# Projections of the next head placed inside a head's attention steps, in a one-core YOCO decoder step

## The reference

```python
k, v = split(rmsnorm(x, kv_norm) @ w_kv)            # 8 heads, keys of 2 x 64, values of 128
q = (rmsnorm(x, norm_mix[1]) @ w_q)                 # 8 heads, 2 maps of 64
for each head h, for both maps c:
    s = q[h, c] @ k[h, c].T * 64 ** -0.5 + bias[h]  # causal; sample rows see the cache and their new keys
    p[c] = softmax(s)
o = (p[0] - lam * p[1]) @ v[h]
o = rmsnorm(o, subln) * (1 - lam_init)
x = x + o @ w_o
x = x + conv_ffn(rmsnorm(x, norm_ffn[1]))
```

## Time and profile before

| | |
|---|---|
| median of 3 runs | 2920.72 us (2919.48 to 2922.08) |
| the profiled execution | 2921.39 us, of which its span is 2919.5 us |
| mean granted TensorE clock | 0.958 |
| PE busy | 2757.5 us (94%) |
| DVE, ACT, POOL busy | 1474.0, 651.8 and 801.0 us |
| keys, values and queries, after their norm | about 1239 to 1519 us of the span |
| attention | 1519 to 1941.3 us |

### The profile page before, as it was taken

One profiled execution on the slowest core, in us unless ns is written; L12 is line 12 of the kernel. 1 busy time (PEld: TensorE's weight loads), 2 busy tenths in 40 slices (PEclk: granted clock), 3 DMA queues, 4 the chain that ended last, 5 costly groups with the idle time before them and its releaser, 6 DMA issues.

```text
span 2919.5 us, 39213 instructions
## 1 busy us (share of the span) xinstructions
PE 2757.5 (94%) x16820; PEld 2678.5 (92%) x16820; DVE 1474.0 (50%) x2348; ACT 651.8 (22%) x946; POOL 801.0 (27%) x456
## 2 busy tenths in 40 slices
PE   5999999999999999899988989879999999999996
PEld 4998999999999999899987778779999999999995
DVE  6666454444445444711315666644544444444556
ACT  4444221111111111300103454432211111111111
POOL 2332333322233223222230011012222332233321
PEclk8999999999999999999997787889999999999998
DMA  3112211111111111123121212021111111111111
GB/s 125 39 42 64 84 44 44 44 51 44 44 44 46 49 44 44 62 84 140 66 83 56 97 56 102 30 101 48 45 45 44 44 45 51 44 44 44 47 48 66
DMA packets 44796, 171.06 MB, mean 59 GB/s; under 512 B 5221, under 2 KB 6821, under 8 KB 44238
## 3 DMA queue, kind: packets, MB, share of 16 engines
q1 hardware_dynamic: 39442, 139.93, 14.4%
q10 hardware_dynamic: 5180, 28.62, 2.6%
HBM read 141.77 MB, written 23.09 MB: 56 GB/s over the span
## 4 chain that ended last, share of the span: by engine, by line
PE 84%; DVE 8%; ACT 4%; issue 3%; POOL 1%; SPq 0%; ACTq 0%; DMA 0%; DVEq 0%; POOLq 0%
PE psum L629 74%; PE psum L865 2%; PE psum L844 2%; PE psum L888 2%; DVE line L1272 2%; DVE x L1338 1%; PE psum L817 1%; PE psum L877 1%; ACT line L1113 1%; ACT probs L1188 1%; DVE line L1313 1%; POOL w_lo L557 0%; DVE inverse_rms L1325 0%; DVE line L1293 0%; DVE xn_lo L1319 0%
## 5 line engine op out<-in xcount | busy, mean ns | idle before, releaser
L629 PE MATMUL psum<-xn_hi,w_hi 128*128 128x352 f32 x3648 | 795.8, 327 | 33.9 <-DVE xn_lo L1319 14.1
L629 PE MATMUL psum<-xn_lo,w_hi 128*128 128x352 f32 x3648 | 790.0, 324 | 0.0
L629 PE MATMUL psum<-xn_hi,w_lo 128*128 128x352 f32 x3648 | 789.6, 325 | 0.0
L553 POOL TENSOR_SCALAR w_hi<-w_raw 128x1024 fp32r<-128x1024 f32 x200 | 215.0, 1075 | 1770.2 <-PE psum L629 1684.4
L629 PEld LDWEIGHTS psum<-xn_hi,w_hi 128*128 128x128 f32 x3648 | 624.3, 190 | 37.6 <-issue 27.3
L629 PEld LDWEIGHTS psum<-xn_lo,w_hi 128*128 128x128 f32 x3648 | 629.2, 189 | 0.0
L629 PEld LDWEIGHTS psum<-xn_hi,w_lo 128*128 128x128 f32 x3648 | 623.0, 189 | 0.0
L557 POOL TENSOR_TENSOR w_lo<-w_raw,w_hi 128x1024 fp32r<-128x1024 f32 x200 | 512.6, 2563 | 16.7
L1338 DVE TENSOR_TENSOR x<-psum,x 128x1056 f32<-128x1056 f32 x208 | 261.3, 1256 | 240.6 <-PE psum L629 239.9
L1113 ACT ACTIVATE line<-line,columns 128x1072 f32<-128x1072 f32 x96 | 123.3, 1285 | 1062.0 <-DVE line L1295 1062.0
L1290 DVE TENSOR_TENSOR line<-psum,inverse_rms 128x704 f32<-128x704 f32 x104 | 92.7, 892 | 472.3 <-PE psum L629 472.2
(11 more groups left out here) (197 smaller groups left out, 2152.3 us busy)
## 6 DMA issues: line engine op xcount, KB each, us to landing
w_raw<-in_w SPq DMA_DIRECT2D x200, 512.0 KB, 3.5
k_pages<-in_cache_k SPq DMA_DIRECT2D x16, 512.0 KB, 4.6
v_pages<-in_cache_v SPq DMA_DIRECT2D x16, 512.0 KB, 5.4
scratch_line<-scratch_row ACTq DMA_DIRECT2D x1, 4608.0 KB, 19.8
x<-in_x ACTq DMA_DIRECT2D x8, 528.0 KB, 11.0
scratch_x<-x ACTq DMA_DIRECT2D x1, 4224.0 KB, 12.1
out_k<-k_t ACTq DMA_DIRECT2D x1, 4224.0 KB, 14.1
out_v<-line ACTq DMA_DIRECT2D x8, 528.0 KB, 2.6
```

The costliest lines, as they stand in the source:

```text
L553: pool.tensor_scalar(WHI[:, s], WRAW[:, s], 1.0, 0.0, ALU.mult, ALU.add).then_inc(w_hi, 1)
L629: last = pe.matmul(PS[:, 3 * (a % 2) + c, 0:CH], w[:, s, k, :], r[:, c * CH:(c + 1) * CH], start=start and first, stop=stop and final)
```

## The change

**The projections.** Units are reordered to query, key, value of one head after another. Only those of head 0's query and key run ahead of attention (`unit(U_A)`, `unit(U_A + 1)`). The other 22 are cut into single k tiles of one chunk: 528 *products* of three matmuls, all on one of the banks 0 and 1, which change after 8 products (`fill`). 16 products run first (`LEAD`), and then 9 in each step (`RATE`), in three groups of three between the step's other work. DVE reads a finished chunk out at two places of a step (`evac_chunks`) into `raw`, from which ACT makes the high parts and POOL the low ones. The second chunk after a finished one may not begin before that one is read (`raw_done`).

**The gains** of the norms are multiplied into the weights by POOL (`split_scaled`), one more two-input instruction of 128 x 1024 for each of the 24 units; `xn_hi` and `xn_lo` are x itself and are computed once. The round trip of queries and keys through `q_t` and `k_t` falls away.

**The steps** are 64, 8 for each head, with tiles in the order 0, 7, 1, 6, 2, 5, 3, 4. `scores` takes both maps by turns in each product. Scores have banks 2 to 5, and all else (transposes, values, sample work) takes banks 6 and 7 by turns in one fixed order (`ring_order`, `open_event`). The maximum and its negation become a minimum of negated scores, so L1727 falls away, and squares are summed by ACT tile by tile.

**Sample attention** treats all 8 sequences of one head at a time: 1 matmul with the new keys and 8 with the pages, three transposes, and 1 and 16 matmuls for the output. Its keys and values come in 32 DMAs of 64 KB for a head in place of 4 of 512 KB.

**The end.** Outputs of heads go to DRAM and come back into `xn_lo`, and the output projection of the first two units runs k tile by k tile (`project`) between the last steps' work.

```diff
-U_K = U_F0 + F_UNITS
-U_V = U_K + KT
-U_Q = U_V + KT
-U_O = U_Q + KT
+U_A = U_F0 + F_UNITS
+U_O = U_A + 3 * NH
...
+TILES = (0, 7, 1, 6, 2, 5, 3, 4)
+STEPS = NH * 8
+LEAD = 16
+RATE = 9
+PRODUCTS = (3 * NH - 2) * NCH * KT
...
+def ring_order():
+    order = []
+    for g in range(STEPS + 3):
+        h, t = divmod(g, 8)
+        if 2 <= g < STEPS + 2:
+            order += [("w", g - 2, b) for b in range(halves(g - 2))]
+        if g < STEPS and t == 2:
+            order += [("v", h, 0), ("v", h, 1), ("v", h, 2)]
+        if g < STEPS and t in (1, 3, 5):
+            order.append((("scores", "weights", "output")[t // 2], h))
+        if g >= 3:
+            order.append(("o", g - 3))
+        if g < STEPS and h and t >= 6:
+            order.append(("ot", h - 1, t - 6))
+        if g == STEPS:
+            order.append(("squares",))
+    return order + [("ot", NH - 1, 0), ("ot", NH - 1, 1)]
...
-        TILES = (0, 1, 2, 3, 4, 5, 6, 7)
-        SAMPLE_STEP = (1, 9)
...
+                pool.tensor_tensor(WRAW[:, s], WRAW[:, s],
+                                   COL[:, gain:gain + KT].unsqueeze(2).to_broadcast([P, KT, P]),
+                                   ALU.mult).then_inc(w_gain, 1)
+                pool.wait_ge(w_gain, n + 1)
+                pool.tensor_scalar(WHI[:, s], WRAW[:, s], 1.0, 0.0, ALU.mult, ALU.add
+                                   ).then_inc(w_hi, 1)
+                pool.wait_ge(w_hi, u + 1)
+                pool.tensor_tensor(WLO[:, s], WRAW[:, s], WHI[:, s].bitcast(F32), ALU.subtract
+                                   ).then_inc(w_lo, 1)
...
+            def low_qk(n):
+                h, k = divmod(n, 3)
+                hi, lo = ((QHI, QLO), (KHI, KLO))[k]
+                pool.wait_ge(qkh_done, 2 * h + k + 1)
+                pool.tensor_tensor(lo[h % 2][:, :], RAW[n % 2][:, 0:SEQ], hi[h % 2][:, :].bitcast(F32),
+                                   ALU.subtract).then_inc(qkl_done, 1)
...
+            def fill(n):
+                for j in range(pos[0], min(pos[0] + n, PRODUCTS)):
+                    q, k = divmod(j, KT)
+                    m, c = divmod(q, NCH)
+                    if j == 0:
+                        wait_read(pe, A_A)
+                    if q >= 2 and k == 0:
+                        pe.wait_ge(raw_done, q - 1)
+                    if c == 0 and k == 0:
+                        pe.wait_ge(w_lo, U_A + 2 + m + 1)
+                    s, cols = (U_A + m) % 2, slice(c * CH, (c + 1) * CH)
+                    pe.matmul(PS[:, q % 2, 0:CH], WHI[:, s, k, :], XNH[:, k, cols],
+                              start=(k == 0), stop=False)
+                    pe.matmul(PS[:, q % 2, 0:CH], WLO[:, s, k, :], XNH[:, k, cols],
+                              start=False, stop=False)
+                    last = pe.matmul(PS[:, q % 2, 0:CH], WHI[:, s, k, :], XNL[:, k, cols],
+                                     start=False, stop=(k == KT - 1))
+                    if k == KT - 1:
+                        last.then_inc(chunk_done, 1)
+                pos[0] = min(pos[0] + n, PRODUCTS)
...
+            def open_event(*e):
+                if EV[e] >= 2:
+                    pe.wait_ge(ev_free[EV[e] % 2], EV[e] // 2)
+                return bank(e)
...
+            def scores(g):
+                h, t = divmod(g, 8)
+                i, p = tile_of(g), h % 2
+                n = (i + 1) * P
+                if t == 0:
+                    pe.wait_ge(qkl_done, 2 * h + 2)
+                if g:
+                    pe.wait_ge(ttr_done, 2 * g)
+                for b in range(0, n, 512):
+                    w = min(512, n - b)
+                    for j, (q, k) in enumerate(((QHI, KHI), (QLO, KHI), (QHI, KLO))):
+                        for c in range(2):
+                            rows = slice(c * HD, (c + 1) * HD)
+                            last = pe.matmul(PS[:, 2 + 2 * c + b // 512, 0:w],
+                                             q[p][rows, i * P:(i + 1) * P], k[p][rows, b:b + w],
+                                             start=(j == 0), stop=(j == 2))
+                            if j == 2 and b + w == n:
+                                last.then_inc(s_done, 1)
...
+            def turn_weights(g):
+                pe.wait_ge(wc_done, g + 1)
+                for half in range(halves(g)):
+                    z = open_event("w", g, half)
+                    for b in range(4 * half, min(4 * half + 4, tile_of(g) + 1)):
+                        last = pe.transpose(PS[:, z, (b % 4) * P:(b % 4 + 1) * P],
+                                            PR0[g % 4][:, b * P:(b + 1) * P], IDENT[:, :])
+                    last.then_inc(ev_done, 1)
...
-                        for c in range(2):
-                            pe.wait_ge(ttr_done, hp * 32 + (2 * t + c + 1))
-                            rows = slice(c * HD, (c + 1) * HD)
-                            for b in range(0, n, 512):
-                                w = min(512, n - b)
-                                for p, (q, k) in enumerate(((QHI, KHI), (QLO, KHI), (QHI, KLO))):
-                                    last = pe.matmul(PS[:, 2 * c + b // 512, 0:w],
-                                                     q[s][rows, i * P:(i + 1) * P],
-                                                     k[s][rows, b:b + w],
-                                                     start=(p == 0), stop=(p == 2))
-                            last.then_inc(s_done, 1)
...
+            fill(LEAD)
+            for g in range(STEPS):
+                h, t = divmod(g, 8)
+                scores(g)
+                fill(RATE // 3)
+                if g >= 2:
+                    turn_weights(g - 2)
+                if t == 2:
+                    turn_values(h)
+                fill(RATE // 3)
+                if t == 1:
+                    sample_scores(h)
+                if t == 3:
+                    sample_weights(h)
+                if t == 5:
+                    sample_output(h)
+                if g >= 3:
+                    values(g - 3)
+                fill(RATE - 2 * (RATE // 3))
+                if h and t >= 6:
+                    turn_output(h - 1, t - 6)
+            turn_weights(STEPS - 2)
...
+            turn_weights(STEPS - 1)
+            pe.wait_ge(raw_done, PRODUCTS // KT)
+            pe.wait_ge(ttr_done, 2 * STEPS)
+            pe.wait_ge(osl_done, 1)
+            project(range(0, 2))
+            values(STEPS - 2)
+            project(range(2, 4))
+            values(STEPS - 1)
+            project(range(4, NH - 1))
+            turn_output(NH - 1, 0)
+            turn_output(NH - 1, 1)
+            project((NH - 1,))
+            for s in range(2, KT):
+                unit(U_O + s, A_O + s, release=(s == KT - 1))
...
+            def evac_chunks(upto):
+                for q in range(taken[0], upto):
+                    m, c = divmod(q, NCH)
+                    n = m + 2
+                    cols = slice(c * CH, (c + 1) * CH)
+                    if c == 0:
+                        line_free(n)
+                    dve.wait_ge(chunk_done, q + 1)
+                    if n % 3 == 0:
+                        dve.scalar_tensor_tensor(RAW[n % 2][:, cols], PS[:, q % 2, 0:CH], -HD ** -0.5,
+                                                 RINV[:, cols], MUL, MUL).then_inc(raw_done, 1)
+                    else:
+                        dve.tensor_tensor(RAW[n % 2][:, cols], PS[:, q % 2, 0:CH], RINV[:, cols], MUL
+                                          ).then_inc(raw_done, 1)
+                taken[0] = max(taken[0], upto)
...
+            for g in range(STEPS):
+                h, t = divmod(g, 8)
+                if g >= 4:
+                    output_rows(g - 4)
+                if t == 2:
+                    sample_biased(h)
+                if t == 4:
+                    sample_combined(h)
+                if t == 6:
+                    sample_rows(h)
+                biased(g)
+                evac_chunks(chunks_by(g, RATE // 3))
+                if g:
+                    combine(g - 1)
+                if t == 1:
+                    sample_biases(h)
+                if t == 3:
+                    sample_normalized(h)
+                if h and t == 4:
+                    variance(h - 1)
+                if h and t == 5:
+                    scaled(h - 1)
+                if g == STEPS - 2:
+                    wait_event_read(dve, "output", NH - 1)
+                    dve.memset(CARRY[:, 5:6], 0.0).then_inc(osm_done, 1)
```

1073 lines of the change are left out of this document (556 added, 517 removed).

## The result

The changed kernel takes 2786.72 us (median of 4 runs, 2785.28 to 2791.95) against 2921.14 us before (a fourth run is added to the three above): a ratio of 0.9545, 95% interval 0.953 to 0.9559. The prediction was 2798 us. On a second chip the same kernel took 2793.94 us (2790.20 to 2794.29), ratio 0.9567 (0.9554 to 0.958). The profiled execution took 2785.28 us with a span of 2783.5 us, 136.0 less than before.

The account below looks back on a forecast made before the run. PE, busy for 94% of the span, bounds the kernel; attention loses time to waits and a lowered clock. The changed stretch's terms sum to 629.0 us against 752.6; 123.6 saved from 2921.4 gives 2798 us, range 2760 to 2872.

Parts of the forecast that it names:

- leading products, first chunk's reading: Before attention's steps: 16 leading products take 7.8 us, and the first chunk's reading, which nothing covers, takes 2.
- seven heads: Attention heads with products: 70.7 us each (68.9 of PE work, 1.8 of waits and delays), 494.9 in all.
- step with the last 8 products: Attention's step holding the remaining 8 products, after the seven heads: 8.4 us.
- last seven steps: Attention steps with no products left run as before: 47.9 x 7/8 = 41.9, less 2 for maps' turns, 40 us.
- the end: After the last steps: 6 us wait, late passes 4.7, two output projection units 23.3, last turn 1, split 2.5: 37.5.
- the fourth step's 1 us for the sample's weights: In a head's fourth step PE wants the sample's weights before DVE has them ready; 1 us of wait shows.
- the copy's 0.3: In each head the third event of `v` makes PE wait 0.3 us for an ACT copy.
- the first rival: Heads with products: PE still waits for weights and rows; in full 84.0 us a head, 2891 us; chance 0.13.
- The second: Heads with products: the clock stays low, 2907 us at 0.82, 2847 halfway, taken as its time; chance 0.11.
- The third: Scores: taking maps by turns brings nothing, since they overlap already; 18 us back, 2816 us; chance 0.07.
- The fourth: Chunk readings on DVE come late behind POOL instructions; 66 chunks cost 169 us, 2967 us; chance 0.06.
- The fifth: Products: a chunk's matmuls on one bank each wait for the one before; 261 us more, 3059 us; chance 0.01.

Follow-up runs that it names:

- nine_at_once: The changed kernel with each step's nine products in one piece behind the scores and chunks read out at the step's end: 2830.16 us, ratio 0.9692.
- maps_in_order: The changed kernel with each step's scores taking all of the first map before the second, as the kernel before does: 2808.52 us, ratio 0.9624.

## Why the prediction was right, step by step

The mechanism was right: products between the pieces of a step cover the waits in the heads, and the clock stays up with them. The 2798 us were 11 too many, and that they are so near is in part luck: the heads came out 19 us below their term, and the last head and the end 11 above theirs.

| term | forecast us | measured us |
|---|---|---|
| first unit and norm gap | 25.1 | 25.0 |
| second unit | 13.3 | 13.4 |
| leading products, first chunk's reading | 9.8 | 7.7 |
| seven heads | 494.9 | 475.9 |
| step with the last 8 products | 8.4 | 6.3 |
| last seven steps | 40.0 | 44.9 |
| the end | 37.5 | 43.5 |
| sum | 629.0 | 616.7 |

**Heads, 19 us too high.** Head 0, which has no outputs of a head before it to turn, took 64.5, the others 68.5 to 68.7. The terms of head 2, each summed from the distances between starts: waits were put at 1.8 us and are 0; the fourth step's 1 us for the sample's weights and the copy's 0.3 did not show. Value passes were put at 0.12 each and cost 0.106 (7.66 for 72), and with the transposes and the sample's output it is 17.6 us for 19.3. Scores are 8.8, of which 0.7 is tile 3 at the low clock (1.58 us where four blocks took 0.91), so 8.1 for 9.2. The 216 matmuls of products take 38.4, of which 0.8 is the low clock (four starts 0.29 apart and not 0.16, and two entries that are longer by 0.1 and 0.2), so 37.6 for 36.7: a group's entry cost 0.11 us and not 0.07. The forecast had nothing for the clock, which cost 1.5. Together 70.7 - 1.8 - 1.7 - 1.1 + 0.9 + 1.5 = 68.5.

**The last head and the end, 11 us too low.** The last seven steps and the end, in the columns of the earlier trace rows:

```profile
1742.20:1787.10 44.90, 35.70 (x231) 27.84 (x230) 29.52 (x90) 29.27 (x71) 3.42 (x2) 0.87 0.46 180
1787.10:1830.60 43.50, 35.18 (x194) 33.76 (x194) 13.00 (x21) 9.88 (x21) 3.50 (x3) 0.83 0.17 58
```

The last seven steps were read off as seven eighths of an old head. That was right for PE's work (43.2 x 7/8 less 2 is 35.8, and it was busy for 35.7) and wrong for its waits: seven eighths of the old head's 4.7 idle us are 4.1, and here they are 9.2. 2.8 of them are for the sample's weights in the fourth step, 3.1 for rows. For the end it is the other way round. Its waits are 2.4, 3.0, 2.0 and 1.0, together 8.4, and the forecast gave 6 and 2.5 for the split. But its work took 35.1 us in place of 29.0: the clock is 0.83 there, and the forecast priced all of it at full clock.

**The rivals.** The chain stayed hidden; nine_at_once, where 18.9 us of waits come back, shows that it is hidden by the groups of three, which was the argument against the first rival. The second, a clock that stays low, is left as the 1.5 us a head at a clock of 0.98. The third is excluded by maps_in_order, where scores cost 2.3 us a head more. The fourth needed 1.87 us of stall a chunk and has one of 1.2 us in all; DVE is busy for 33 us of 68.5 in a head, as was worked out (ACT for 28.8, where about 35 were). The fifth: matmuls of a group start 0.16 us apart on one bank. The gain's multiplication on POOL, priced at 2.56 us, took 1.9.

**The rules.** That matmuls start in strict program order (the Trainium skill, TensorE: Matmul & The Clock Gate, The mechanism) would make the smaller tiles slower in maps_in_order; they were not. Its 2808.52 us lies nearer to the 2805 of four tiles than to the 2823 of eight; the total was taken on another chip and says little by itself, but the heads say it: 2.3 us each, all in the larger tiles.

## What to carry to other kernels

Work that depends on nothing around it is worth most when it is cut into pieces and put between two neighbours that hand a bank to each other: the same 72 products a head gave 475.9 us in 24 pieces, 511.0 in 8 and 534.0 in 3. A saving on the busiest engine counts in full only where nothing else is waited for, so cover the chain first and shorten the engine's work then (for the same edit, 2.3 us a head where products cover the chain, and 10.2 us for all eight heads, 1.3 each, in the kernel before). Price the stretch that has no filler left by itself: it is where the waits collect.

## What the runs showed of the hardware

TensorE's granted clock fell while PE was busy without a gap: in each of the seven heads it went to 1.2 GHz right behind 32 records of 4 columns, and stayed at 2.4 GHz in all seven when these were left out. Cut in four parts with one product between, they brought it down still, in seven of seven; with two or three between, it fell in none, one and three of the seven heads in three profiles of the same order. It did not fall each time that they ran in one piece either: in maps_in_order one of the seven heads kept the full clock behind the same 32 records.

```profile
1328.50:1397.80 69.30, 69.22 (x469) 62.29 (x468) 32.94 (x103) 28.13 (x78) 21.36 (x11) 1.00 0.25 78
```

What decides between the two these runs do not show.

Scores of two maps on 64 rows each overlap by turns at 1.59 us for twelve records of 512 columns (0.13 us each), where one map alone takes 0.19 a record (0.57 for three), and where the maps stand one after the other, the second map's first record starts beside the third of the first map's six (both at 1405.21), and so ahead of the last three, which come before it in the program.
